# Eight weight chunks get their rounded high parts from a DMA that Pool issues, not from a copy on ScalarE

## What is computed

```python
h = rms_norm(x, norm_mix_g[i])
proj = h @ w_in[i]
ca, cg, q, k, v, iq, ik, iw, z, xbc, dt = jnp.split(proj, SPLITS, axis=-1)
...
x = x + jnp.concatenate([u, att, y], axis=-1) @ w_out[i]
h = rms_norm(x, norm_ffn_g[i])
f = causal_dwconv(h @ w_up[i], ffn_conv_w[i], ffn_conv_b[i])
fa, fg = jnp.split(f, 2, axis=-1)
x = x + (jax.nn.silu(fg) * fa) @ w_down[i]
```

## Time and profile before

| | us |
|---|---|
| median of 3 runs | 715.89 (715.77 to 715.96) |
| the profiled execution | 716.0 |
| its span in the trace | 714.2 |
| PE busy in the span | 696.5 (98%) |
| DVE busy | 544.6 (76%) |
| ACT busy | 380.9 (53%) |
| Pool busy | 139.3 (19%) |

### The profile page before, as it was taken

How to read it: one execution, slowest core, us unless ns; L and a number is a source line. 1 busy time by engine, 2 the same in 40 slices (tenths; PEclk the granted TensorE clock), 3 DMA queues, 4 the chain that set the end, 5 groups by cost and what they waited for, 6 DMA issues and landing times.

```text
span 714.2 us, 9787 instructions
## 1 busy us (share of the span) xinstructions
PE 696.5 (98%) x3402; PEld 560.1 (78%) x3402; DVE 544.6 (76%) x852; ACT 380.9 (53%) x570; POOL 139.3 (19%) x114
## 2 busy tenths in 40 slices
PE   4999999999999999999999999999999999999998
PEld 4776888767677788788888888888888888888886
DVE  5368979977898967677667777876766766997895
ACT  6354655988878765633464344343243333654660
POOL 2000478844464302233410000000000000000000
PEclk9999999999999999999999999999999999999999
DMA  8731314222111142312235578666688547864542
GB/s 244 225 138 61 118 59 119 60 60 69 50 60 60 60 178 73 134 60 61 67 111 154 176 229 250 202 169 194 184 250 244 181 157 297 296 220 143 167 163 88
DMA packets 87555, 104.10 MB, mean 146 GB/s; under 512 B 6872, under 2 KB 65592, under 8 KB 87520
## 3 DMA queue, kind: packets, MB, share of 16 engines
q1 hardware_dynamic: 87375, 103.12, 46.0%
q10 hardware_dynamic: 144, 0.52, 0.2%
HBM read 87.10 MB, written 16.54 MB: 145 GB/s over the span
## 4 chain that ended last, share of the span: by engine, by line
PE 83%; ACT 7%; DVE 5%; issue 2%; POOL 2%; DMA 1%; DVEq 0%; ACTq 0%; POOLq 0%
PE bank L1767 72%; PE bank L1773 4%; PE bank L1787 2%; ACT tapped L1129 1%; ACT w_hi L934 1%; POOL u_acc L860 1%; PE bank L1975 1%; DVE u_acc L622 1%; PE bank L2031 1%; PE bank L1951 1%; DVE xbcT L1427 1%; PE bank L1926 1%; ACT prob L1052 1%; DMA x_in<-in_x 1%; DVE w_lo L640 1%
## 5 line engine op out<-in xcount | busy, mean ns | idle before, releaser
L1767 PE MATMUL bank<-h_hi,w_hi 128*128 128x512 f32 (+1 forms) x496 | 192.9, 389 | 0.0
L1767 PE MATMUL bank<-h_lo,w_hi 128*128 128x512 f32 (+1 forms) x496 | 189.9, 383 | 0.0
L1767 PE MATMUL bank<-h_hi,w_lo 128*128 128x512 f32 (+1 forms) x496 | 189.8, 383 | 0.0
L1767 PEld LDWEIGHTS bank<-h_hi,w_hi 128*128 128x128 f32 x496 | 93.2, 188 | 25.5 <-issue 7.8
L1621 DVE SCALAR_TENSOR_TENSOR f<-bank,prm,f 128x511 f32<-128x511 f32 x88 | 65.8, 748 | 60.9 <-ACT f L1182 55.4
L1767 PEld LDWEIGHTS bank<-h_hi,w_lo 128*128 128x128 f32 x496 | 93.2, 188 | 18.5
L1767 PEld LDWEIGHTS bank<-h_lo,w_hi 128*128 128x128 f32 x496 | 93.3, 188 | 17.4
L860 POOL TENSOR_TENSOR u_acc<-tapped,u_acc 128x511 f32<-128x511 f32 (+29 forms) x60 | 87.8, 1463 | 47.8 <-ACT tapped L1129 44.6
L1182 ACT ACTIVATE f<-bank,prm 128x512 f32<-128x512 f32 x44 | 34.2, 777 | 70.5 <-PE bank L1767 70.3
L640 DVE TENSOR_TENSOR w_lo<-w_raw,w_hi 128x2048 fp32r<-128x2048 f32 x24 | 55.7, 2322 | 7.7 <-ACT w_hi L934 7.6
L1767 PE MATMUL bank<-w_hi,g_parts 128*128 128x512 f32 x168 | 53.8, 389 | 0.0
(11 more groups left out here) (279 smaller groups left out, 1227.5 us busy)
## 6 DMA issues: line engine op xcount, KB each, us to landing
w_raw<-in_w_up SPq DMA_DIRECT2D x44, 512.0 KB, 6.1
w_raw<-in_w_in SPq DMA_DIRECT2D x34, 512.0 KB, 4.6
down_raw<-in_w_down SPq DMA_DIRECT2D x22, 512.0 KB, 5.4
weight_sums<-down_raw SPq DMA_DIRECT2D x11, 768.0 KB, 5.3
w_raw<-in_w_out SPq DMA_DIRECT2D x12, 512.0 KB, 4.2
weight_sums<-w_sum SPq DMA_DIRECT2D x11, 512.0 KB, 2.7
w_raw<-weight_sums SPq DMA_DIRECT2D x6, 768.0 KB, 6.4
down_raw<-weight_sums SPq DMA_DIRECT2D x5, 768.0 KB, 5.9
```

The lines of the kernel that those rows point to most:

```text
L1767: ins = pe.matmul(o, a, b, start=first and i == 0 and q == 0, stop=last and i == n - 1 and q == 2)
```

## The change

For chunks 8 to 15 (`CAST`) ACT no longer copies. At the step `("hi", c)` Pool waits until PE has finished chunk c-2 and then issues two DMAs of 512 KB that read the same weights from HBM again and write them, rounded to float32r, straight into `whi`. ACT at the same step waits until both have landed and adds one to `w_hi_ready`. The raw chunk is still loaded by SP, since the low part needs it; DVE waits for it in addition. The halves of a chunk and their patterns are as for the raw load (`parts_of_chunk` holds what stood in `load`).

```diff
+CAST = range(8, 16)
...
+        cast_landed = [sem(f"cast_landed{i}") for i in range(NSLOT)]
...
             eng.wait_ge(w_hi_ready, c + 1)
+            if c in CAST:
+                eng.wait_ge(w_landed[c % NSLOT], 32 * (c // NSLOT + 1))
...
+                for dst, src in parts_of_chunk(c, slot):
+                    sp.dma_start(dst, src).then_inc(done, 16)
...
+                elif k == "hi" and s[1] in CAST:
+                    c = s[1]
+
+                    pool.wait_ge(acc_step, STEP[("chunk", c - NSLOT)])
+                    for dst, src in parts_of_chunk(c, whi[:, c % NSLOT, :]):
+                        pool.dma_start(dst, src).then_inc(cast_landed[c % NSLOT], 16)
...
             def split_hi(c):
+                if c in CAST:
+                    act.wait_ge(cast_landed[c % NSLOT], 32 * ((c - CAST[0]) // NSLOT + 1))
+                    act.sem_inc(w_hi_ready, 1)
+                    return
                 act.wait_ge(w_landed[c % NSLOT], 32 * (c // NSLOT + 1))
```

More of the change, by code:

```diff
@@ L641, in part_lo, with parts_of_chunk @@
                               whi[:, slot, cols].bitcast(F32), ALU.subtract).then_inc(ready, 1)
+        def parts_of_chunk(c, slot):
+            what, i = CHUNKS[c]
+            if what in ("iq", "xbc"):
+                c0 = C_IQ if what == "iq" else C_XBC + 256 * i
+                src = w_in[:, c0:c0 + 256].rearrange("(k p) n -> p k n", p=P)
+                dst = slot.rearrange("p (k n) -> p k n", k=KD)
+                return [(dst[:, a:a + 4], src[:, a:a + 4]) for a in (0, 4)]
+            if what in ("conv", "up"):
+                w, ca, cg = (w_in, C_CA, C_CG) if what == "conv" else (w_up, 0, D_FF)
+                dst = slot.rearrange("p (k s n) -> p k s n", k=KD, s=2)
+                return [(dst[:, :, s], w[:, c0 + P * i:c0 + P * i + P]
+                         .rearrange("(k p) n -> p k n", p=P)) for s, c0 in enumerate((cg, ca))]
+            if what == "out":
+                src = w_out[P * MIX_TILE[i[0]]:P * (MIX_TILE[i[0]] + 4),
+                            512 * i[1]:512 * i[1] + 512]
+            else:
+                c0 = {"q": C_Q, "k": C_K, "v": C_V, "z": C_Z}[what]
+                src = w_in[512 * i:512 * i + 512, c0:c0 + 512]
+            src = src.rearrange("(k p) n -> p k n", p=P)
+            dst = slot.rearrange("p (k n) -> p k n", k=4)
+            return [(dst[:, a:a + 2], src[:, a:a + 2]) for a in (0, 2)]
         @block.sync
@@ L646, in load @@
             def load(c):
-                what, i = CHUNKS[c]
                 if c >= NSLOT:
```

## The result

The changed kernel takes 725.51 us (median of 4, 725.25 to 728.06) against 715.91: a ratio of 1.014, 95% interval 1.013 to 1.0155, or 9.6 us. The forecast was slower, 729.5, with a range of 717.5 to 749. The side was right, the time lay in the range, and the forecast was 4 us too high.

What follows compares the result with a forecast made beforehand. PE, busy 696.5 of 714.2 us, bounds the kernel, but up to about 143 the chain runs through Pool's taps and ACT. Landing delays at X = 8 sum to 13.6 us, giving 729.5; range 717.5 to 749.

Steps and rivals of the forecast that it cites:

- The bound of 2.9 us: PE's waits from 95 to 270 total 2.9 us, claimed as the most the change could gain.
- X: Time from the start of Pool's first issue to the second half's landing; taken as 8.0 us, ends 5.3 and 10.4.
- the issue: Pool's two DMA issues per chunk, taken as 3.3 us from its inverse roots of eight elements.
- the rival that rested on it: Quick landing: rounded halves land as fast as raw ones, 713.0 to 715, or about as before by the skill; chance 0.12.
- The steps of chunks 8 to 11: Late landings block ACT (DVE at chunk 8); PE's total lateness grows to 4.2, 5.9, 7.3 and 10.6 us.
- the same sum: Chunk-by-chunk sum over chunks 8 to 15 of landing delays reaching PE; 13.6 us at X = 8.
- a sign against me only if it came alone: Listed among signs of being wrong: a PE wait for w_lo at chunk 8 alone; no size given.
- The slope: One us of X is worth some 6 us of the kernel, since the chunks' delays add up.
- 1.7 + 0 + 1.0 + 0.3 = 3.0 us: PE delays claimed for chunks 12, 13, 14 and 15 from landings later than the old copies' ends, at X = 8.
- the edits taken at nothing: Priced at zero: DVE's added wait, 8 MB more from HBM, Pool's later taps; SP's queue untouched.
- the case that I had priced: A DVE low part running during Pool's issue holds up its descriptors; X would grow by up to 2.3 us.
- the lock for the descriptors: Shared-port lock: DVE might hold up Pool's descriptors; by the skill nothing was added and the sum stayed 13.6.

Runs made afterwards that it cites:

- 719.34 in both kernels: Chunks 12 to 15 alone converted, and the kernel before with Pool waiting plus one inverse root and no ACT copies at those chunks, no DMA: 719.34 each.
- the dead DMAs: Kernel before plus Pool's wait and rounding DMAs for chunks 12 to 15, landing in spare DRAM nobody reads, ACT's copies kept: 717.06 us.
- the one with a root in their place: Kernel before plus Pool's wait and one eight-element inverse root at chunks 12 to 15, no DMA, ACT's copies kept: 716.95 us.
- the kernel with these four: The changed kernel with only chunks 8 to 11 converted, 12 to 15 copied by ACT as before: 724.32 us.
- the kernel with the early issues for all eight chunks: The changed kernel with chunk 8's issues ahead of Pool's three inverse roots and chunk 9's ahead of tap 12: 728.86 us.

## Why the prediction was right, and where it was not

**What bounds the kernel.** Right. Over the whole run ACT's copies are hidden; without four of them 1.8 us come back. The bound of 2.9 us for all eight is not contradicted, though only half was tried. I then priced the removed copies at nothing while ACT is blocked. As a saving that was right; as a disturbance it was wrong: they also kept the products, and so Pool's taps, where they collided less.

**X was mis-sized:** 8.0 taken, 5.5 to 6.8 measured, nearer to the lower end. The term that was wrong is the issue: 3.3 us by the rows of Pool's inverse roots, 1.5 to 1.8 measured. An arithmetic instruction of Pool says nothing of its DMA issue; SP's 0.92 us for two was the nearer row. From the start of its own issue the second DMA of a pair took 4.6 to 5.9 us to land, against 4.6 for the raw loads. The Trainium skill ("DMA: Bandwidth & Descriptors", section "Anatomy of one DMA — SWDGE (gpsimd) path") gave an estimate of 4.4 us for the pair; the trace has 1.1 to 2.4 more, and the rival that rested on it did not come.

**The steps of chunks 8 to 11** held in kind. With the measured X in the same sum, PE is 1.7 late after the landing of chunk 8 (1.9 measured), 3.1 after that of chunk 9 (3.8 to 4.3), 3.3 after 10 (5.5) and 4.5 after 11 (8.7). The remainder at 10 and 11 is in the main the clock, some 3 us in the profiled execution, and Pool's own time. The waits that I named came: ACT 4.88 us idle at chunk 9 for "some 6", PE on kT, probT and prob for 9.3 us where I had said about 14; at chunk 8 w_lo was the wait. I had listed that one as a sign against me only if it came alone.

**The slope** was said to be 6 us per us of X over eight chunks. Over four it is 4.1, of which 2.2 is waiting and the rest the lower clock; my sum goes from 2.3 to 10.6 us at chunk 11 for 2.7 us of X, 3.1 per us. The sum had no term for the clock. Over eight chunks the slope wasn't run.

**Chunks 12 to 15: the right size for the wrong reason.** The sum gave 1.7 + 0 + 1.0 + 0.3 = 3.0 us by late landings. The loss is 3.4, but it is there with no DMA at all (719.34 in both kernels), and it stands elsewhere: at chunk 12, for which the sum had 1.7, PE wins 0.8 back in the changed kernel, and chunk 13, "without a delay", costs 1.2. That the two totals agree is luck. The step that failed stands under the edits taken at nothing: "Pool's later taps: after chunk 11 it waits for ACT more than it works". True, and no argument, since the time when a tap runs counts, not only whether Pool has time. Alone it cost 1.0 us, with the freed ACT 3.4.

**The shared port.** Pool's issues were not held up where they could be watched: those of chunks 13 to 15 took 1.5 us with a two-input instruction of DVE (xbcT) beside them for 1.2 to 1.3 of it, and with the dead DMAs the kernel took the time of the one with a root in their place. No low part ran during an issue, so the case that I had priced never came. Whether the landing is held up stays open: with the same pattern (chunks 12 to 14) X was 5.8 to 6.5 us, and nothing here says why. But I had weighed the lock for the descriptors only, and had read it one way, DVE holding up Pool. The runs show both: low parts of 3.0 us for 2.28, four DVE taps in 5.45 us for 2.93. That agrees with the same section of the Trainium skill ("SBUF — State Buffer", "SBUF: two separate sides") read to its end: whichever of the two instructions starts first has the shared pair for its whole length.

**Two errors in the sum partly cancelled.** With the right X it would have given 4.5 us, or 720.4: too low by 5. What it then lacked is 3.4 us of DVE and Pool in chunks 12 to 15, 1.3 of Pool's time in chunks 8 to 11, and some clock (1.6 in the median of the kernel with these four). These and the landing's 5.4 make 11.7, while the whole change costs 9.6; the halves overlap by 2.1 us, and which part gives way when both are present was not tried. Nor do the whole change's executions order by clock as clearly: 725.25, 725.41 and 725.61 at 0.998, 1.000 and 0.997; only 728.06 at 0.995 stands apart.

## What to carry to other kernels

A copy that the bounding engine hides is cheap where it stands, and what replaces it must be priced by when its engine may start it and by who stands behind the wait, for each chunk: here 5.5 to 6.8 us of latency against -1.5 to 8.0 us of room. An engine with idle time still has a schedule: 1.6 us at each of four chunks on Pool, idle four fifths of the run, cost 1.0 us, and freeing ACT beside it, which alone gave 1.8 us, turned that into 3.4; by the traces both move instructions of Pool and DVE onto each other. When two edits are measured apart, run them together before calling the remainder a third cause.

## What the runs showed of the hardware

- A pair of 512 KB DMAs that round to float32r, issued by Pool, occupied Pool for 1.65 to 1.83 us (chunks 8 to 10) and 1.45 to 1.56 (11 to 15), and landed 5.5 to 6.8 us after the start of the first (5.2 to 7.6 over all the kernels of the experiments).
- An addition on Pool and a two-input instruction on DVE stretch one another: 2.28 to 3.0 us for a low part on DVE, 1.3 to 3.0 for a tap on Pool, 2.93 to 5.45 for four taps on DVE. The one under way when the other began kept its length (1.26 us, 2.28 us).
- In the changed kernel PE's clock fell to 1.2 GHz for 3.41 us at a time after PE had stood still for 1.6 to 1.9 us once or twice. A standstill alone doesn't tell: in the kernel with the early issues for all eight chunks the clock fell after one of 2.62 us and stayed at 2.4 GHz after one of 2.58. A kernel whose executions differ in it shows groups, 1.1 us apart (717.2 and 718.3) in one case.
